# Where VectorE takes the gate of the convolution in a hybrid decoder step

## What is computed

```python
def ssd_branch(z, xpad, dt_raw, h0, segments, conv_w, conv_b, dt_bias, a_log, d_skip, norm_g):
    xa = jax.nn.silu(causal_conv(xpad, conv_w, conv_b))
    ...
    xs = xa[..., :SSD_WIDTH].reshape(b, t, SSD_HEADS, SSD_HEAD_DIM)
    Bm = xa[..., SSD_WIDTH:SSD_WIDTH + gn].reshape(b, t, SSD_GROUPS, D_STATE)
    Cm = xa[..., SSD_WIDTH + gn:].reshape(b, t, SSD_GROUPS, D_STATE)
    ...
    y = y + d_skip.astype(jnp.float32)[:, None] * xs.astype(jnp.float32)
    y = y.reshape(b, t, SSD_WIDTH) * jax.nn.silu(z.astype(jnp.float32))
```

## Time and profile before

| | us |
|---|---|
| median of 3 runs | 2078.48 |
| lowest and highest | 2077.53, 2079.0 |
| the profiled execution, its own time | 2081.84 |
| its span, first to last instruction | 2080.1 |
| TensorE busy in the span | 1984.8 (95%) |
| VectorE busy | 1195.2 (57%) |
| POOL busy, ScalarE busy | 636.8, 625.6 |

### The profile page before, as it was taken

The page is one execution under the profiler, slowest core; times in us unless marked ns, Lnnn a source line. Parts: engine busy times, 40 slices in busy tenths (PEclk is TensorE's granted clock), DMA queues, the critical chain, the costliest instruction groups (busy, mean ns, idle before and its releaser), DMA issues. The chain is left out here.

```text
span 2080.1 us, 35138 instructions
## 1 busy us (share of the span) xinstructions
PE 1984.8 (95%) x13151; PEld 1597.2 (77%) x13151; DVE 1195.2 (57%) x2028; ACT 625.6 (30%) x1313; POOL 636.8 (31%) x582
## 2 busy tenths in 40 slices
PE   8999999958998999999999899999999999999998
PEld 4566666635666777777777688899989998899887
DVE  4566776655763766666676655454444444444444
ACT  2233323224443444444444522211111111111110
POOL 1244433440003633333333532522322232223211
PEclk9999999978998999999999999999999999999999
DMA  6011111156321104332233211210222012201202
GB/s 227 19 42 39 38 38 38 34 131 146 104 68 40 21 21 153 104 79 64 66 79 93 93 42 32 81 54 10 60 60 60 14 46 60 60 26 35 60 20 82
DMA packets 180702, 132.05 MB, mean 63 GB/s; under 512 B 61773, under 2 KB 165502, under 8 KB 180454
## 3 DMA queue, kind: packets, MB, share of 16 engines
q1 hardware_dynamic: 179398, 129.38, 21.7%
q0 software_dynamic: 144, 1.08, 0.2%
q10 hardware_dynamic: 1040, 0.00, 0.0%
HBM read 110.81 MB, written 19.65 MB: 63 GB/s over the span
## 5 line engine op out<-in xcount | busy, mean ns | idle before, releaser
L2646 PE MATMUL sm_ps<-nT_hi,f_gu_hi 128*128 128x344 f32 x1056 | 338.2, 320 | 2.9 <-DVE f_e L2605 2.5
L2646 PE MATMUL sm_ps<-nT_hi,f_gu_lo 128*128 128x344 f32 x1056 | 337.5, 320 | 0.0
L2646 PE MATMUL sm_ps<-nT_lo,f_gu_hi 128*128 128x344 f32 x1056 | 337.4, 320 | 0.0
L1832 POOL TENSOR_TENSOR s_b_latT<-s_b_latT_hi,s_b_latT_lo 128x1024 f32<-128x1024 f32 x64 | 153.9, 2405 | 327.1 <-DVE s_b_latT_lo L1904 327.1
L1931 DVE TENSOR_REDUCE s_b_ssq<-s_b_ksq 128x8 f32<-128x512 f32 x256 | 172.4, 684 | 115.5 <-ACT s_b_ksq L1776 113.5
L1776 ACT ACTIVATE s_b_ksq<-sm_ps 128x512 f32<-128x512 f32 x256 | 153.1, 598 | 204.0 <-PE sm_ps L2024 166.8
L2024 PE MATMUL sm_ps<-s_b_wk_hi,s_b_latT_hi 128*128 128x512 f32 x512 | 207.2, 405 | 5.3 <-ACT s_b_ksq L1776 5.2
L2646 PEld LDWEIGHTS sm_ps<-nT_hi,f_gu_hi 128*128 128x128 f32 x1056 | 199.1, 189 | 4.1 <-DVE f_e L2605 2.8
L2024 PE MATMUL sm_ps<-s_b_wk_hi,s_b_latT_lo 128*128 128x512 f32 x512 | 200.6, 392 | 0.0
L2024 PE MATMUL sm_ps<-s_b_wk_lo,s_b_latT_hi 128*128 128x512 f32 x512 | 200.0, 391 | 0.0
L2646 PEld LDWEIGHTS sm_ps<-nT_lo,f_gu_hi 128*128 128x128 f32 x1056 | 198.6, 188 | 0.4
(11 more groups left out here) (375 smaller groups left out, 3556.5 us busy)
## 6 DMA issues: line engine op xcount, KB each, us to landing
p_latn<-in_cache_kv_latent SPq DMA_DIRECT2D x256, 128.0 KB, 2.0
gu_raw<-in_w_gate SPq DMA_DIRECT2D x22, 512.0 KB, 4.2
gu_raw<-in_w_up SPq DMA_DIRECT2D x22, 512.0 KB, 5.3
f_wd_raw<-in_w_down SPq DMA_DIRECT2D x11, 1024.0 KB, 5.1
t_w_in<-in_w_in SPq DMA_DIRECT2D x8, 980.0 KB, 10.6
t_x<-in_x_prompt SPq DMA_DIRECT2D x8, 512.0 KB, 4.6
p_krn<-in_cache_k_rope SPq DMA_DIRECT2D x256, 16.0 KB, 1.8
w_raw<-in_w_out SPq DMA_DIRECT2D x8, 512.0 KB, 6.5
```

Of the source, the lines that this page charges most:

```text
L1832: out(pool.tensor_tensor(out=flat(latT), in0=flat(latT_hi).bitcast(F32), in1=flat(latT_lo).bitcast(F32), op=ALU.add), "sum_done")
L2646: ins = pe.matmul(ps[:, bank + j, 0:W], w[fi][:, j, k, :], x[:, k, cols], start=(k == 0 and w is gu_hi and x is nT_hi), stop=(k == KD - 1 ...
```

## The change

The three instructions of the gate leave the start of VectorE's iteration and become a function `silu(t)`. It is called for tile 0 right behind the convolution of tile 0, ahead of that tile's first step. For the other tiles `silu(t + 1)` is called in the iteration of tile t, between the two sums for q and k and the scan's first output `yo`. No other engine's code changes, and no instruction is added or taken away.

```diff
+        def silu(t):
+            R = rows(t)
+            dve.wait_ge(S["conv_exp"], t + 1)
+            add_one_reciprocal(ex[:, :, 0:R])
+            out(dve.tensor_tensor(out=conv[:, :, 0:R], in0=conv[:, :, 0:R], in1=ex[:, :, 0:R], op=ALU.mult), "conv_silu")
+
         def iteration(t, p, ahead, after_it):
...
                                          op0=ALU.add, op1=ALU.subtract), "dt_w")
-            dve.wait_ge(S["conv_exp"], t + 1)
-            add_one_reciprocal(ex[:, :, 0:R])
-            out(dve.tensor_tensor(out=conv[:, :, 0:R], in0=conv[:, :, 0:R], in1=ex[:, :, 0:R], op=ALU.mult), "conv_silu")
             dve.wait_ge(S["cl_rstd"], t + 1)
...
             out(dve.tensor_reduce(stq[0:R, 0:H], qsq[0:R, :, :], AXX, ALU.add), "qk_sums")
+            if after_it:
+                silu(t + 1)
             dve.wait_ge(S["yo_ready"], t + 1)
...
         convolve(0, 0)
+        silu(0)
         iteration(0, 0, True, True)
```

## The result

| | before | changed |
|---|---|---|
| median of 4 runs each | 2078.74 us | 2091.93 us |
| lowest, highest | 2077.53, 2080.4 | 2090.39, 2094.07 |
| span of the profiled execution | 2080.1 | 2090.7 |
| ratio of the runs | | 1.0054 (95%: 1.0041 to 1.0067) |

The kernel became slower: by 0.54% or some 11.2 us by the recorded ratio, by 10.6 us by the spans, and by 13.2 us (0.63%) by the two medians, which also lies within the interval. The forecast was 11.4 us, or 2089.9, with a range up to 2093.5; the measured median stands 2.0 us above the forecast. Before any cause is named, here is where the time went by the two traces. I set a mark at the start of the second state step in each tile (L735 before, L740 after), since TensorE's last wait of a tile stands behind it.

A forecast was written before the change was run, and what follows sets the result against it. TensorE, busy 94% of a tile, was taken as the bound. The terms 8.4 + 1.25 - 0.35 + 0 + 2.1 = 11.4 us put the median at 2089.9 us (+0.55%), range 2085.5 to 2093.5.

The forecast's parts named there:

- term 1: End of tiles 1 to 6: VectorE's idle time absorbs part, the second k transposes start 1.40 us later; 8.4 us lost.
- term 2: End of tile 0: the second k transposes start later by the same spacing; 1.25 us lost.
- term 3: Tile starts: TensorE's gap before the `t_ud` product nearly stays, since `xdt` also holds it; 0.35 us gained, bounds 0 and 1.4.
- term 4: Tiles 7 and 8: tile 7's delay is offset by tile 8 starting without its gate; zero, within -0.3 and +0.5 us.
- term 5: Moved gate beside POOL's work: VectorE may wait up to 0.6 us a tile; half taken, 2.1 us, bounds 0 and 4.2.
- Rival (b): TensorE's clock halves at the new gaps at six tile ends, 1.8 us each: 2100.7 us; chance 0.08.
- Rival (c): Slack later in the tile takes up the delay, less than half of 9.65 us remains: about 2081.5 us; chance 0.08.
- (a): TensorE's gap at tile starts vanishes in full, 11.7 us gained against 9.65 lost: 2076.5 us, faster; chance 0.05.

The follow-up runs named there:

- half_dose: The changed kernel with the gate on only the first three of six blocks, the others left ungated; ratio 0.999 to the kernel before.
- ahead_of_sums: The changed kernel with the next tile's whole gate moved earlier, behind its convolution and ahead of the q and k sums; ratio 0.9981 to the kernel before.
- product_only: The kernel before with the gate in its old place but without add and reciprocal, only the product; ratio 0.9976 to the kernel before.
- after_yo: The changed kernel with the gate one instruction later, behind the scan's first output (yo_taken); ratio 1.0037 to the kernel before.

## Why the prediction was right

- **The idle time takes the first part, TensorE the rest** (term 1). Forecast 1.40 us a tile and 0.3 for POOL, measured 1.65 as the sum of both. The order was as forecast: k product at once behind `y`, state at once behind k, `st` 0.6 us late (0.74), q transposes held by the k product. `half_dose` and `ahead_of_sums` show the mechanism from two sides: less work, or the same work where idle time is, and the loss is gone.
- **Tile 0** (term 2 with its share of POOL): forecast 1.25 + 0.3, measured -0.26 + 1.70 = 1.44 us, when the half clock of the earlier trace rows is taken out.
- **The gap in front stays** (term 3). Right in kind, wrong in size. I took 0.35 us for all tiles; it was 0.28 us in three of them and 0.11 in tile 7, 0.95 in all, within the bound of 1.4. The term was mis-sized because I costed it from the tile of the earlier trace rows, whose gap was 1.46, and laid that on all; that tile was held by `xdt` from the start and gave nothing. The earlier trace rows with its longest of 1.7 us could have told me that in three tiles the wait for `ud` was 1.66, and these fell to 1.38.
- **Tiles 7 and 8 cancel** (term 4). Forecast zero, measured +4.85 - 4.69 = +0.16 us up to tile 8's first transposes. The way there was right as well: the first step of tile 8 was to move by some 4.7 us against the mark of tile 6, and moved by 4.86. Tile 8 itself then took 1.1 us more at half clock, which no term had.
- **POOL** (term 5). Half of the bound was a choice between two outcomes that I took for a near tie, and it came out as that half, but by another way: POOL came first in every tile, yet the product lost 0.29 us and not 0.6. It had started 0.18 us after POOL's, so that 0.43 us of that product lay beside it; why 0.29 of them show was not settled. That the half bet and the loss agree is luck. As forecast, the add in turn delayed POOL's small addition (0.45 us where the earlier trace rows have 0.20).
The Trainium skill, page "SBUF — State Buffer", section "Who interferes with whom", states the exclusive lock and the kinds of instruction that take part in it. On the kinds the traces agree: the reciprocal, with its one input, kept its 4.95 us in every place, and the product with two inputs in SBUF was lengthened only beside POOL. On the size they do not quite: the section has the later one blocked in full, which would be the 0.43 us, and 0.29 was measured.
- **The sum.** For tiles 1 to 6 terms 1, 3 and 5 gave 9.9 us; measured were 3.90 - 2.20 + 7.38 = 9.1. With tile 0's 1.44 and 0.16 at the seam of 7 and 8 that is 10.7. The stretches at half clock (+2.2, -1.7, +1.1) and the start (-1.15) add 0.45 more. So the mechanism accounts for 10.7 of the 11.15 us, and the match with 11.4 owes something to luck, by about half a microsecond, besides the luck in term 5.
- **Rival (b)** did not occur where I put it: the clock stayed at 1.00 in the loop. It did, at a place that I had not looked at, the seam of tiles 0 and 1, in exchange for the stretch that the kernel before has elsewhere. Rival (c) had nothing for it; (a) fell by `product_only`.

## What to carry to other kernels

Work moved ahead costs nothing up to the idle time that lies between its new place and the first wait of the bounding engine (3.3 us of it showed nothing against 4.90 us of idle time), and what goes beyond shows nearly in full (6.45 us, with 0.29 of contention, showed 1.65). So sum the idle times up to that wait and put the work ahead of the earliest of them that its input allows, here ahead of the sums and not behind them. Check also what the delayed instructions feed on other engines: here it was POOL's q product, with 0.31 us to spare. Ahead of a wait that several chains release, take all of them before you promise a gain: with one removed, the next stood 0 to 0.3 us behind. Where an engine has no cover, as in the last tiles, work each end separately: the loss at one (4.85 us) and the gain at the next (4.69 us) were each some three times what a tile of the loop lost.

## What was not expected of the hardware

Each execution profiled has a stretch at half clock within its first 102 us, at places that differ between kernels: at 40 to 48 us, at 63 to 67, or at 91 to 99. Its cost was 1.7 us at one place and 2.2 at another, and in tile 8 the same 12 q products took 4.11, 5.80 or 6.93 us by kernel. So two profiles can differ by more than the work in their kernels does. `after_yo` shows it: 2083.1 us of span in its profile, 7.6 us under the changed kernel, of which tiles 1 to 6 explain 2.7 and tile 8, with its clock, 3.0. What places these stretches was not settled.
